# Moving two projection tiles into the start of the mixer, and writing its first and last steps out by hand

## The reference, cut to what matters

```python
h = rms_norm(x, norm1)
proj = h @ w_in                      # sb_q, sb_k, sb_v, dn_qkv, dn_z, dn_a, dn_b, hg_q, hg_f, hg_i, hg_g
sb_o = stick_breaking_attention(sb_q, sb_k, sb_v)
dn_o = gated_delta_rule(l2_norm(q), l2_norm(k), v, g, beta)   # q, k, v = silu(conv(dn_qkv)); chunks of 64
#   per chunk: solve (I + m) sol = [v_beta, k_beta * exp(gc)], m strictly lower triangular
hg_o = hgrn2_recurrence(silu(hg_q), hg_k, hg_i, log_f)
x = x + concat(sb_o, dn_o * silu(dn_z), hg_o * sigmoid(hg_g)) @ w_out      # each head normalised first
h2 = rms_norm(x, norm2)
x = x + (silu(h2 @ w_gate) * (h2 @ w_up)) @ w_down
return rms_norm(x, final_norm)
```

## Time and profile before

| | us |
|---|---|
| median of 3 runs (lowest, highest) | 1503.9 (1503.65, 1504.33) |
| the profiled execution | 1501.83 |
| its span, first to last instruction | 1500.0 |
| PE busy in the span | 1432.6 (96%) |
| DVE, POOL, ACT busy | 751.9, 651.4, 558.1 |
| mix stretch | 136.7 to 464.0 |
| mixer's first two steps | 465.4 to 500.8 |
| steps 0 to 6 | 500.8 to 686.0 |
| last two steps, with four halves of the output projection | 686.0 to 731.0 |

### The profile page before, as it was taken

One profiled execution on the slowest core, in us unless ns is written; L12 is line 12 of the kernel. 1 busy time (PEld: TensorE's weight loads), 2 busy tenths in 40 slices (PEclk: granted clock), 3 DMA queues, 4 the chain that ended last, 5 costly groups with the idle time before them and its releaser, 6 DMA issues.

```text
span 1500.0 us, 24371 instructions
## 1 busy us (share of the span) xinstructions
PE 1432.6 (96%) x9201; PEld 1195.7 (80%) x9201; DVE 751.9 (50%) x1287; ACT 558.1 (37%) x1317; POOL 651.4 (43%) x607
## 2 busy tenths in 40 slices
PE   5999999999997999998899889999999999999997
PEld 4878888888886888887788768888888888888886
DVE  5005544564554688876123954435435344354446
ACT  5223444443443344443244433242332332423335
POOL 4112323232324656663332565363463553634651
PEclk9999999999998899999999999999999999999999
DMA  5122232333324232313323020211211202112113
GB/s 183 45 55 59 74 95 78 103 82 90 87 72 117 72 104 73 117 56 138 106 85 98 28 57 29 56 57 57 56 38 48 85 29 57 56 57 57 42 44 127
DMA packets 144787, 111.19 MB, mean 74 GB/s; under 512 B 5584, under 2 KB 132128, under 8 KB 144672
## 3 DMA queue, kind: packets, MB, share of 16 engines
q1 hardware_dynamic: 144528, 109.11, 24.0%
q10 hardware_dynamic: 144, 0.52, 0.1%
HBM read 88.63 MB, written 20.99 MB: 73 GB/s over the span
## 4 chain that ended last, share of the span: by engine, by line
PE 87%; DVE 6%; issue 2%; POOL 2%; ACT 1%; DMA 1%; SPq 0%; POOLq 0%; DVEq 0%; ACTq 0%
PE banks L291 10%; PE banks L293 9%; PE banks L292 9%; PE banks L2002 8%; PE banks L2003 8%; PE banks L2004 8%; PE banks L2019 5%; PE banks L2021 5%; PE banks L2020 5%; PE banks L691 2%; PE banks L1022 2%; PE banks L1068 2%; PE banks L1033 2%; PE banks L1014 1%; DVE area L1398 1%
## 5 line engine op out<-in xcount | busy, mean ns | idle before, releaser
L291 PE MATMUL banks<-act_h,w_h 128*128 128x512 f32 x624 | 251.7, 403 | 5.2 <-POOL w_l L283 4.8
L283 POOL TENSOR_TENSOR w_l<-w_raw,w_h 128x1024 fp32r<-128x1024 f32 x49 | 121.1, 2474 | 299.0 <-ACT w_h L279 299.0
L293 PE MATMUL banks<-act_h,w_l 128*128 128x512 f32 x624 | 244.9, 392 | 0.0
L292 PE MATMUL banks<-act_l,w_h 128*128 128x512 f32 x624 | 244.2, 391 | 0.0
L2126 POOL TENSOR_TENSOR w_l<-area,w_h 128x512 fp32r<-128x512 f32 x102 | 141.1, 1388 | 158.3 <-ACT w_h L2039 158.3
L2126 POOL TENSOR_TENSOR w_l<-w_raw,w_h 128x512 fp32r<-128x512 f32 x86 | 118.2, 1378 | 165.2 <-ACT w_h L2039 165.2
L2270 DVE TENSOR_TENSOR area<-area,banks 128x512 f32<-128x512 f32 x176 | 121.0, 687 | 120.7 <-PE banks L2021 118.2
L291 PEld LDWEIGHTS banks<-act_h,w_h 128*128 128x128 f32 x624 | 118.0, 189 | 32.7 <-POOL w_l L283 4.8
L293 PEld LDWEIGHTS banks<-act_h,w_l 128*128 128x128 f32 x624 | 117.8, 189 | 25.8
L292 PEld LDWEIGHTS banks<-act_l,w_h 128*128 128x128 f32 x624 | 118.3, 190 | 22.7
L2002 PE MATMUL banks<-act_h,w_h 128*128 128x512 f32 x320 | 124.6, 389 | 2.9 <-POOL w_l L2126 2.9
(11 more groups left out here) (259 smaller groups left out, 2746.1 us busy)
## 6 DMA issues: line engine op xcount, KB each, us to landing
w_raw<-in_w_in SPq DMA_DIRECT2D x31, 512.0 KB, 4.0
area<-in_x SPq DMA_DIRECT2D x8, 1024.0 KB, 7.8
projected_tm<-area SPq DMA_DIRECT2D x32, 256.0 KB, 3.4
w_raw<-in_w_out SPq DMA_DIRECT2D x16, 512.0 KB, 4.3
w_raw<-in_w_gate SPq DMA_DIRECT2D x12, 512.0 KB, 4.0
area<-in_w_down SPq DMA_DIRECT2D x12, 512.0 KB, 4.0
w_raw<-in_w_up SPq DMA_DIRECT2D x12, 512.0 KB, 4.7
projected_cm<-area SPq DMA_DIRECT2D x20, 256.0 KB, 2.6
```

The source lines that it names most:

```text
L283: e.tensor_tensor(w_l[:, b], w_raw[:, b], w_h[:, b].bitcast(F32), ALU.subtract).then_inc(sems["wl_ready"], 1)
L291: e.matmul(dst, w_h[:, b, k], act_h[:, k, cols], start=(k == 0), stop=False)
L292: e.matmul(dst, w_h[:, b, k], act_l[:, k, cols], start=False, stop=False)
L293: mm = e.matmul(dst, w_l[:, b, k], act_h[:, k, cols], start=False, stop=(k == KT - 1))
```

## The change

1. The tile `plain` (hg_i) leaves `SLOTS`; its two passes stand at the end of `TILES`. The first 22 tiles (NM = 44 halves) are spread over the 48 units: unit k takes pieces `pieces_to(k)` to `pieces_to(k + 1)`, 7 or 8 of them, and `ENDING` says which half ends in a unit. All that follows a half goes by `ended(k - n)`. The order of the slots changes.
2. The last two tiles (4 halves, 32 pieces) are made in the mixer: 12 pieces between the first products of chunk 0, 20 between the levels of its inverse. They have buffers of their own (`late_c`, `late_t`) and use banks 4 and 5. ACT reads them out (`late_taken`), PE turns them (`late_turn`), DVE stages them (`late_staged`), SP stores them ahead of `load_decays(2)`, and `load_rest(0)` waits for these stores.
3. `step(t)` stays for t = 0 to 6, in a new order on PE, ACT, DVE and POOL. First, second, last and end step are functions of their own with their own orders.
4. Tiles W_OUT and W_OUT + 1 are loaded in steps 0 and 1 and split in steps 5 and 6; before, W_OUT was loaded and split in the mix stretch and W_OUT + 1 split in the last but one step. In the last steps `out_product(0)` moves behind `scores(7, 2)`, and `out_taken(2)` moves ahead of the output part.

```diff
+    TILES = [(i, slot) for i in range(2) for slot in SLOTS] + [(i, tile_of("plain", 0, C_HI, 1, I_AT)) for i in range(2)]
+    NM, NH = 4 * len(SLOTS), 2 * len(TILES)
+    def pieces_to(k):
+        return NM * KT * k // NH
+    ENDING = {next(k for k in range(NH) if pieces_to(k + 1) >= KT * (h + 1)): h for h in range(NM)}
 # mix_pe
-                    mix_free(e, k, k % 2)
-                    dense_half(e, W_P1 + k // 2, (W_P1 + k // 2) % 2, k % 2, bank(k % 2))
+                    for piece in range(pieces_to(k), pieces_to(k + 1)):
+                        h, first = divmod(piece, KT)
+                        if first == 0:
+                            mix_free(e, h, h % 2)
+                        dense_part(e, W_P1 + h // 2, (W_P1 + h // 2) % 2, h % 2, bank(h % 2), first, first + 1)
 # mixer_sync
             def load_rest(c):
+                for half in range(2):
+                    e.wait_ge(sems[f"tm_stored{half}"], 16 * (before(TOKM, NH) // 2))
...
+                if t == -1:
+                    for k in range(NM, NH):
+                        store_tok(e, k, late_t)
+                if t in (0, 1):
+                    load_tile(e, W_OUT + t, (W_OUT + t) % 2, out_tile(t))
 # mixer_pe
+            def late_dense(k, piece):
+                w = W_P1 + k // 2
+                if piece == 0 and k >= NM + 2:
+                    mix_taken(e, k - 2)
+                dense_part(e, w, w % 2, k % 2, bank(4 + k % 2), piece, piece + 1)
+            def first_step():
+                late_dense(NM, 0)
+                key_key(0)
+                late_dense(NM, 1)
...
+                late_dense(NM + 1, 1)
+                key_query(0)
+                m_turn(0)
+                late_dense(NM + 1, 2)
+                late_dense(NM + 1, 3)
+            def second_step():
+                late_dense(NM + 1, 4)
+                pack(0, 1)
+                late_turn(NM)
+                late_dense(NM + 1, 5)
+                turn(0, 0)
+                late_dense(NM + 1, 6)
+                update(0, 1)
+                late_dense(NM + 1, 7)
+                late_dense(NM + 2, 0)
+                pack(0, 2)
...
+                late_dense(NM + 3, 7)
+                m_turn(1)
+                update(0, 6)
+                late_turn(NM + 3)
             def step(t):   # new order, in full:
+                key_state(t)  turn(u, 0)  pack(u, 1)  scores(t, 0)  update(u, 1)  new_values(t)  pack(u, 2)  turn(u, 1)
+                query_state(t)  update(u, 2)  mix_turn(s, 0)  turn(u, 2)  pack(u, 3)  scores(t, 1)  update(u, 3)
+                query_intra(t)  turn(u, 3)  pack(u, 4)  mix_turn(s, 1)  update(u, 4)  scores(t, 2)  turn(u, 4)  pack(u, 5)
+                state_update(t)  update(u, 5)  scores(t, 3)  turn_keys(t)  turn(u, 5)  pack(u, 6)  gated_state(t)
+                key_key(v)  gated_out(t)  m_turn(v)  update(u, 6)  key_query(v)
+            def last_step():
+                scores(7, 0)  key_state(7)  mix_turn(6, 0)  scores(7, 1)  new_values(7)  query_state(7)  query_intra(7)
+                scores(7, 2)  out_product(e, 0)  scores(7, 3)  mix_turn(6, 1)  out_product(e, 1)  gated_out(7)
+            def end_step():
+                mix_turn(7, 0)  out_product(e, 2)  mix_turn(7, 1)  out_product(e, 3)
 # mixer_dve, step(t), new order in full
+                log_sigmoids(u)  pack(u, 1)  residual(t)  update(u, 1)  take(t, 0)  running(u)  gated_state(s)  take(t, 1)
+                pack(u, 2)  update(u, 2)  final_hg(s)  queries(u, 0)  queries(u, 1)  pack(u, 3)  apart(v)  update(u, 3)
+                final_sb(t)  low(s, 0)  take(t, 2)  pack(u, 4)  take(t, 3)  queries(u, 2)  update(u, 4)  take(t, 4)
+                take(t, 5)  pack(u, 5)  lengths(t)  low(s, 1)  new_state(t)  update(u, 5)  take(t, 6)  queries(u, 3)
+                take(t, 7)  queries(u, 4)  queries(u, 5)  pack(u, 6)  with_decay(v)  final_dn(t)  queries(u, 6)
+                update(u, 6)  pack(v, 0)  update(v, 0)  scores(v)
 # mixer_pool, step(t), new order in full
+                unit(v)  [t == 5: split_low(W_OUT)]  spread(u, 0) to spread(u, 4)  keys(u, 0)  values(u)  spread(u, 5)
+                gates(t)  spread(u, 6)  keys(u, 1)  [t == 6: split_low(W_OUT + 1)]  keys(u, 2)  keys(u, 3)  keys(u, 4)
+                decayed_queries(u)  causal(u)  decayed_keys(u)  from_start(u)  keys(u, 5)  keys(u, 6)  to_end(u)
 # mixer_act, second_step, start
+                late_taken(NM)  softplus(0)  inverse(0, 0)  spans(0, 0, 3)  late_taken(NM + 1)  inverse(0, 1)
 # mixer_act, last steps
+                high(6, 0)  gated_squares(6)  new_values(7)  gated_lengths(6)  squares(7)  high(6, 1)  out_taken(e, 0)  lengths(7)
+                out_taken(e, 1)  gated_squares(7)  high(7, 0)  gated_lengths(7)  high(7, 1)  out_taken(e, 2)
```

More of the change, by code:

```diff
@@ L1183, in step @@
[L1183 to L1186, removed]
+                key_state(t)
+                turn(u, 0)
+                pack(u, 1)
+                scores(t, 0)
+                update(u, 1)
+                new_values(t)
+                pack(u, 2)
+                turn(u, 1)
+                query_state(t)
+                update(u, 2)
                 if live(s):
                     mix_turn(s, 0)
-                if live(u):
-                    pack(u, 3)
@@ L1191, in step @@
[L1191 to L1206, removed]
+                turn(u, 2)
@@ L1207, in step @@
+                pack(u, 3)
+                scores(t, 1)
+                update(u, 3)
+                query_intra(t)
+                turn(u, 3)
+                pack(u, 4)
                 if live(s):
                     mix_turn(s, 1)
[L1209 to L1217, removed]
@@ L1231, in step @@
+                pack(u, 5)
+                state_update(t)
+                update(u, 5)
+                scores(t, 3)
+                turn_keys(t)
+                turn(u, 5)
+                pack(u, 6)
+                gated_state(t)
                 if live(v):
                     key_key(v)
-                if live(t):
-                    gated_out(t)
+                gated_out(t)
+                if live(v):
+                    m_turn(v)
+                update(u, 6)
                 if live(v):
@@ L1389, in mixer_act, with last_step @@
-            for t in TIMES:
-                if t == -1:
-                    e.wait_ge(sems["zeroed"], 1)
-                if t == 0:
-                    e.wait_ge(sems["zeroed"], 4)
+                whole_inverse(u)
+                inverse(u, 5)
+            def last_step():
+                high(NT - 2, 0)
+                gated_squares(NT - 2)
+                new_values(NT - 1)
+                gated_lengths(NT - 2)
+                squares(NT - 1)
+                high(NT - 2, 1)
+                out_taken(e, 0)
+                lengths(NT - 1)
@@ L1394, in mixer_act, with end_step @@
+            def end_step():
+                out_taken(e, 1)
+                gated_squares(NT - 1)
+                high(NT - 1, 0)
+                gated_lengths(NT - 1)
+                high(NT - 1, 1)
+                out_taken(e, 2)
+            first_step()
+            e.wait_ge(sems["zeroed"], 1)
+            second_step()
+            e.wait_ge(sems["zeroed"], 4)
+            for t in range(NT - 1):
                 step(t)
+            last_step()
+            end_step()
         def mixer_dve(e):
@@ L1550, in final_sb, with late_staged, first_step, second_step @@
                 final(c, SBH, pb[:, SB_AT - 2 * DNW:], r_sb[:, c, :], SBD, 0, gain_row[:, 0:SBW], "fin_sb")
+            def late_staged(k):
+                stage_tok(e, k, late_t)
+            def first_step():
+                apart(0)
+                with_decay(0)
+                pack(0, 0)
+                update(0, 0)
+                scores(0)
+            def second_step():
+                log_sigmoids(0)
+                running(0)
+                pack(0, 1)
+                update(0, 1)
+                late_staged(NM)
+                pack(0, 2)
+                queries(0, 0)
+                update(0, 2)
+                late_staged(NM + 1)
+                pack(0, 3)
+                update(0, 3)
+                pack(0, 4)
+                update(0, 4)
+                queries(0, 1)
+                apart(1)
+                pack(0, 5)
+                queries(0, 2)
+                scores(1)
+                update(0, 5)
+                queries(0, 3)
+                queries(0, 4)
+                with_decay(1)
+                late_staged(NM + 2)
+                queries(0, 5)
+                pack(0, 6)
+                queries(0, 6)
+                pack(1, 0)
+                update(0, 6)
+                update(1, 0)
+                late_staged(NM + 3)
@@ L1611, in step @@
[L1611 to L1619 removed]
+                new_state(t)
+                update(u, 5)
+                take(t, 6)
+                queries(u, 3)
+                take(t, 7)
+                queries(u, 4)
+                queries(u, 5)
@@ new lines, in step, with last_step @@
```

(42 more changed lines are left out.)

542 lines of the change are left out of this document (291 added, 251 removed).

## The result

| | us |
|---|---|
| changed kernel, median of 19 runs (lowest, highest) | 1507.7 (1497.5, 1514.9) |
| kernel before, median of 19 runs beside them | 1503.3 (1501.6, 1504.3) |
| ratio, 95% interval | 1.0028 (1.0018 to 1.0039) |
| forecast | 1480, range 1467 to 1491 |

What follows compares the result with a forecast made beforehand. PE was taken to set the pace, with its waits and half-clock stretches as the places to gain. -16.1 + 0 + 1.8 - 9.3 = -23.6 us from 1503.9 gave 1480.3, say 1480, range 1467 to 1491.

Steps and rivals of the forecast that it cites:

- part 3: New order of steps 0 to 6: 8.9 us of waits go, 9.8 new at final_sb beside gates, 0.9 added: +1.8 us.
- part 4: Last steps: two PE waits (9.3 us) and 1.5 us at half clock go, 1.5 us new wait: -9.3 us, -11 to -6.
- rival d: Second step: the clock stays at half throughout, 39 us more for PE: 1519 us; chance 1 in 100.
- (a): Steps 0 to 6: gates does not meet final_sb, so they gain 8.0 us: 1470.5 us; chance 0.26.
- (b): Second and last steps: dense pieces fill less, DVE and ACT set the second step's pace: 1492 us; chance 0.15.
- (c): Middle steps: the DVE and POOL lock makes DVE the pace, deciding from 3.6 us a step: 1510; 0.05 with (d).
- Part 1: Two tiles moved from the mix stretch into the inverse of chunk 0: -16.1 us, between -18 and -13.
- Part 2: Mix stretch: 44 halves spread over 48 units, PE keeps the pace: cost 0, at most 2 us.
- the feared wait for the weights of W_OUT + 3: Last steps, ahead of mix_turn(7, 1): a new PE wait behind the late load and split, 1.5 us, from 0 to 4.

Runs made afterwards that it cites:

- e1: Changed kernel with final_sb(t) on DVE moved behind update(u, 4), as it stood before: 1474.5 us, ratio 0.9809.
- e3: Changed kernel with 6 unused 128x128 matmuls on PE ahead of update(u, 4), where it waits: 1480.5 us, ratio 0.9856.
- e5b: Kernel before the change, with two unused 128x1664 copies on DVE ahead of pack(u, 4) to make PE wait: 1527.8 us, ratio 1.0164.
- e8: Changed kernel with final_sb(t), the W_OUT + 1 split and queries(u, 5) moved, and the two tiles back in the mix stretch: 1483.8 us, 0.9882.
- e9: Changed kernel with final_sb(t), the W_OUT + 1 split and queries(u, 5) moved, and the last two steps in the old order: 1478.3 us, 0.9838.
- e7: Changed kernel with 3 unused matmuls on PE ahead of update(u, 4), filling only some of the wait: 1490.5 us, ratio 0.9921.

## Why the prediction was wrong

**The step that failed is part 3.** It ends with "So steps 0 to 6: -8.9 + 9.8 + 0.9 = +1.8 us, between -8.9 and +9." Measured: +33.4. The mechanism was in it: `final_sb` beside `gates`, and a wait ahead of `update(u, 4)` in each of 7 steps. The wait was even well sized: 1.4 us a step forecast, 12.3 / 7 = 1.76 measured; `final_sb` with 1.4 us more than its 0.86, measured 2.52; and a step of 25.8 us without the meeting, measured 25.9 in e1. What is missing is that such a wait lowers the clock, as e1, e3 and e5b show together. That term is 29.1 us and has no place in the sum, neither in the likeliest case nor in a bound. The bounds were also off by a little: with 0 and 2.5 us a step the sum of part 3 runs from -8.0 to +9.5.

The trace of before had two hints. In the last steps the clock fell within waits of 4.5 and 4.6 us and stayed at half for 6.8 us (first row), which I counted as a gain of part 4 only. And in the inverse of chunk 0, behind the wait of 5.2 us, it stayed at half for 26.6 us, with PE busy 21.1 of them and no wait longer than 0.6 but one of 1.2 (second row):

```profile
701.40:708.20 6.80, 4.08 (x21) 3.47 (x22) 4.99 (x15) 0.41 (x2) 0.97 (x1) 0.50 0.24 78
...
472.90:499.50 26.60, 21.12 (x296) 19.23 (x294) 9.93 (x30) 7.86 (x18) 16.08 (x31) 0.50 0.34 113
```

The 8.9 us of waits of at most 1.0 us in the steps had left the clock at 1.00. Between 1.0 and 4.5 us the mixer at full clock had no row, so a new wait of 1.4 to 2.5 us had an unknown price: nothing, or a stretch at half clock. I wrote "a stretch without waits has nothing that lowers it" for the second step (rival d), and did not ask the same of part 3, where I had just put a wait. With one stretch of the 6.8 us seen, a step would lose an estimated 3.4 us, 7 steps 24 us, and the range would have reached 1491 + 24 = 1515. The stretches that came were up to 13.7 us long.

**The rivals.** (a), no meeting, 1470.5, is what e1 made true: 1474.5, and 1467 with the two other moves. (b) did not come: the second step has 0.8 us of waits. (c), slower by the lock between DVE and POOL, named the place and the right threshold of 3.6 us a step, and the steps grew by 33.4 / 7 = 4.8; but it saw DVE becoming the pace. DVE is busy 163.0 of 218.6 us; it was PE's clock. (d) had the right mechanism in the wrong stage.

**Part 1** was right with its sum: -16.1 forecast, -14.7 by the start of `key_state(0)`, 17.8 by e8. The region took 42.8 us from 443.3, inside the 40 to 43 of the forecast. **Part 2**, at 0: one wait of 0.3 us in the mix stretch. **Part 4** was right: -9.3 forecast, -10.9 in the profile, 12.3 by e9; the stretch to half 4 took 34.1 us for 36, since the feared wait for the weights of W_OUT + 3 did not appear.

**The rule of the Trainium skill** (SBUF — State Buffer, "Who interferes with whom") held and was the right thing to weigh against the change: of the four operations of `final_sb` the first took 0.27 us, and the other three, 1.28, 0.77 and 0.43 us, each ended 0.1 us behind the end of another operation of POOL. The Trainium skill (TensorE: Matmul & The Clock Gate, "What's actually happening") would have helped here too: it states that a hardware block sets PE's clock to 1.2 or 2.4 GHz by how busy PE has been recently. The rows of steps 2 and 3 agree, with a granted clock of 1.00 or 0.50 and its fall behind a wait.

## What to carry to other kernels

Price a wait of PE by what stands behind it as well as by its length: among small matmuls, a wait of 1.5 to 1.8 us cost 4 us more in slower matmuls in the mean (29.1 / 7), and work without a use in the gap was cheaper than the gap. Whether such a wait costs less among dense matmuls no run here shows. When an order is laid out by durations, keep DVE operations with two SBUF inputs away from long POOL operations, and look for the meeting in the trace by the mean of the same operation (0.2 us alone, 0.6 beside POOL). A change that moves the time little can still hold a gain of 26 us: compare the stages before giving it up.

## What the runs showed of the hardware that I had not expected

- Each of the seven waits of 1.5 to 1.8 us between small matmuls was followed, 0.1 to 2.5 us after its end, by a stretch at 1.2 GHz: 3.4 us in two steps, 10.3 in one and 13.6 to 13.7 in four, in steps 2 and 3 after a course that had been alike up to then. Waits of 0.8 to 1.2 us did it in five of seven steps of one execution (e7) and not in the two others; waits of up to 1.0 us, scattered, did not in the steps of the kernel before. What decides between them stays open.
- Four short DVE operations in a row did not wait once for POOL: the last three of `final_sb` were each held by another operation of POOL, 2.52 us in all for 0.86.
- Scatter between runs of one kernel (1497.5 to 1514.9 us in 19 runs) went with such waits; e3, with more work and no wait over 0.7 us in its steps, had 1479.9 to 1483.8 in four. That the two belong together is argued, not shown; e8, whose profile has no wait over 0.7 us in its steps either, had one run of 1491.4 beside three of 1483.1 to 1484.3.
